# Order of VectorE's work between the expert chunks: the mixer's slices first, each routing step one chunk earlier

## The reference, cut to what matters

```python
def peer_ffn(xn, w_query, sub_keys, peer_u, peer_v):
    q = (xt @ w_query).reshape(t, PEER_HEADS, 2, PEER_HALF)
    sk = jnp.einsum('thcd,ckd->thck', q, sub_keys)
    top_s, top_i = lax.top_k(sk, PEER_TOPK)            # 16 of 128 keys, twice
    cand_s = top_s[:, :, 0, :, None] + top_s[:, :, 1, None, :]
    best_s, best_pos = lax.top_k(cand_s, PEER_TOPK)    # 16 of 256 pairs
    idx = jnp.take_along_axis(cand_i, best_pos, axis=-1)
    gate = jax.nn.softmax(best_s, axis=-1)
    h = einsum('thkd,td->thk', peer_u[idx], xt)
    return einsum('thk,thkd->td', gate * gelu(h), peer_v[idx])
x = x + y @ w_out                                      # end of the mixer
x = x + peer_ffn(rms_norm(x, norm2_g), w_query, sub_keys, peer_u, peer_v)
```

## Time and profile before

| what | value |
|---|---|
| median of 3 runs | 2962.0 us |
| profiled execution | 2951.57 us, span of its instructions 2949.8 us |
| busy: TensorE, VectorE, ScalarE, GpSimd | 2097.7, 2065.5, 1041.2, 1194.0 us |
| moved by DMA | 1173.26 MB, of which the gathers 1073.81 MB and the queue of weights 97.07 MB |
| first gather issued | at 160.3 us, the last at 2927.1 us |
| chain of work that ended last | gathers in flight 48%, TensorE 22%, VectorE 18% |

### The profile page before, as it was taken

The page is one execution under the profiler, slowest core; times in us unless marked ns, Lnnn a source line. Parts: engine busy times, 40 slices in busy tenths (PEclk is TensorE's granted clock), DMA queues, the critical chain, the costliest instruction groups (busy, mean ns, idle before and its releaser), DMA issues.

```text
span 2949.8 us, 37238 instructions
## 1 busy us (share of the span) xinstructions
PE 2097.7 (71%) x12696; PEld 1036.4 (35%) x12696; DVE 2065.5 (70%) x5215; ACT 1041.2 (35%) x3347; POOL 1194.0 (40%) x1028
## 2 busy tenths in 40 slices
PE   8888787777777876586775877667776665656565
PEld 7554454344443432243342533234343111111111
DVE  2466678977567687867567678976766766777665
ACT  2322345633233455423223345632223222222222
POOL 0034334443344334444343434543444444444443
PEclk9988999888888987888887988889898678677768
DMA  6189999999999999999999999999999999999998
GB/s 233 36 345 418 419 419 419 395 420 419 419 419 419 420 414 414 417 384 420 420 420 420 416 386 420 421 386 419 420 420 421 421 421 421 418 418 420 419 415 341
DMA packets 174350, 1173.26 MB, mean 398 GB/s; under 512 B 19280, under 2 KB 19408, under 8 KB 43088
## 3 DMA queue, kind: packets, MB, share of 16 engines
q0 software_dynamic: 147456, 1073.81, 87.8%
q1 hardware_dynamic: 26704, 97.07, 8.4%
HBM read 1168.71 MB, written 2.10 MB: 397 GB/s over the span
## 4 chain that ended last, share of the span: by engine, by line
DMA 48%; PE 22%; DVE 18%; ACT 5%; issue 5%; POOL 1%; SPq 0%; DVEq 0%; POOLq 0%; ACTq 0%
DMA gather<-experts,idx 48%; PE ysum L686 12%; DVE gather L1259 9%; PE bank L466 6%; ACT amp L915 2%; POOL gather L421 1%; ACT diag L923 1%; PE ysum L474 1%; PE bank L661 1%; ACT gel L908 1%; DVE x L1235 1%; PE bank L515 1%; DVE shared L1045 0%; DVE scratch L1206 0%; DVE scratch L1210 0%
## 5 line engine op out<-in xcount | busy, mean ns | idle before, releaser
L421 POOL DMA_INDIRECT gather<-experts,idx x1024 | 1193.8, 1166 | 1733.8 <-PE ysum L686 1411.5
L686 PE MATMUL ysum<-gather,diag 64*64 64x512 f32 x8192 | 1263.2, 769 | 728.3 <-ACT diag L923 696.7
L1259 DVE CUSTOM_DVE_ANT_0 gather<-gather,xc 128x1024 f32<-128x1024 f32 x1024 | 1229.8, 1224 | 682.8 <-DMA gather<-experts,idx 680.0
L686 PEld LDWEIGHTS ysum<-gather,diag 64*64 64x64 f32 x8192 | 365.7, 172 | 1526.9 <-ACT diag L923 906.8
L908 ACT ACTIVATE gel<-hdot 128x4 f32<-128x4 f32 x255 | 52.4, 205 | 1679.4 <-DVE hdot L1259 1679.4
L466 PE MATMUL bank<-xnT,w 128*128 128x256 f32 (+1 forms) x2048 | 467.1, 384 | 5.9 <-DVE xnT L975 5.9
L466 PEld LDWEIGHTS bank<-xnT,w 128*128 128x128 f32 x2048 | 380.0, 194 | 100.6 <-issue 42.8
L923 ACT ACTIVATE diag<-cc,amp 128x64 f32<-128x64 f32 x1020 | 267.9, 333 | 0.0
L915 ACT ACTIVATE amp<-gel,gate 128x1 f32<-128x1 f32 x1020 | 216.8, 283 | 8.3
L908 ACT ACT_TABLE_LOAD x105 | 134.7, 1283 | 1.8
L661 PEld LDWEIGHTS bank<-w,yT 128*128 128x128 f32 x768 | 87.3, 192 | 17.8 <-issue 17.8
(11 more groups left out here) (126 smaller groups left out, 1490.2 us busy)
## 6 DMA issues: line engine op xcount, KB each, us to landing
w<-weights SPq DMA_DIRECT2D x164, 512.0 KB, 7.9
gather<-experts,idx POOLq DMA_INDIRECT x1024, 15.1
gather<-weights SPq DMA_DIRECT2D x4, 1024.0 KB, 5.6
y_out<-x SPq DMA_DIRECT2D x4, 512.0 KB, 7.8
x<-x_in SPq DMA_DIRECT2D x2, 512.0 KB, 5.3
g2b<-g_rows SPq DMA_DIRECT2D x2, 512.0 KB, 11.7
x<-x_in SPq DMA_DIRECT2D x1, 1024.0 KB, 12.4
cc<-consts_in SPq DMA_DIRECT2D x1, 920.5 KB, 6.4
```

The source lines that it names most:

```text
L421: pool.indirect_dma_start(gather[:, n % SLOTS, :], None, uv_d[m // 2], bass.IndirectOffsetOnAxis(ap=idx[:, g % 2, k:k + 1], axis=0)).then_ ...
L686: mm = nc.tensor.matmul(ysum[outs, q * 512:(q + 1) * 512], diag[toks, n % NDIAG, :], gather[toks, n % SLOTS, DM + hf * 512:DM + (hf + 1) * ...
L1259: e = V.tensor_tensor_reduce(out=gather[:, n % SLOTS, 0:DM], in0=gather[:, n % SLOTS, 0:DM], in1=xc[:, :], scale=1.0, scalar=0.0, op0=ALU. ...
```

## The change

The routing step moves from ahead of the `yield` to behind it. On VectorE the order becomes: dot products of c, add_tile if due, slices of c, routing step, dot products of c + 1. And the steps of head g + 1 are assigned to other chunks: with g = cg // 4 + 1, `route_experts(g)` stands behind the slices of chunk 0 of head g - 1, `route_gate(g)` behind those of chunk 2, `route_keys(g + 1)` behind those of chunk 3. Only head 1, at the start, has its keys at chunk 0 and its experts at chunk 1 as before. The numbers and kinds of instructions do not change. The other engines' programs are as they were.

```diff
@@ peer_dve
-                head = c // 4
...
                     add_tile(cg // per_tile - 1)
-                nm, nh = divmod(m * TT * HEADS + head + 1, TT * HEADS)
-                if nm < NBLK:
-                    if c % 4 == 0:
-                        route_keys(dve, nm, nh)
-                    elif c % 4 == 1:
-                        route_experts(dve, nm, nh)
-                    elif c % 4 == 3:
-                        route_gate(dve, nm, nh)
-                yield
+                yield
+
+                g = cg // 4 + 1
+                route = lambda step, to: step(dve, *divmod(to, TT * HEADS)) if to < NBLK * TT * HEADS else None
+                if cg == 0:
+                    route(route_keys, g)
+                elif cg == 1 or c % 4 == 0:
+                    route(route_experts, g)
+                elif c % 4 == 2:
+                    route(route_gate, g)
+                elif c % 4 == 3:
+                    route(route_keys, g + 1)
             if m == NBLK - 1:
                 add_tile(m * TT + 1)
```

## The result

The changed kernel takes 2965.47 us (median of 7 runs, 2963.11 to 2970.89), the kernel before 2960.65 us in runs of the same session (7 runs, 2955.64 to 2963.01). The ratio is 1.002, with a 95% interval of 1.0011 to 1.0029. That is some 5 us: within the 0.3% that the forecast called no change and within its range, but the interval leaves one out, and the sign is not the one of the sum (-0.9 us). So there is a small loss to explain.

What follows compares the result with a forecast made beforehand. The DMA engines were taken to bound the kernel. The terms summed to -0.9 us, taking the runs' median of 2962.0 to 2961, and unplaced small waits to 2960.0 us; the range was 2944 to 2973.

Steps and rivals of the forecast that it cites:

- What bounds the kernel: Whole stream: the DMA engines bound it, so engine order can win only the time they lack work, 26.7 us.
- block 1's chunk 32: Slices ahead of the keys step let TensorE's spread start earlier: 2.5 us of gain, between 0 and 3.95.
- 1050 to 1240: Stretch of scattered dips losing 2.7 us, relieved ahead of chunk 2: taken as -1 us, between -2.7 and +3.
- the stretch 530 to 600: VectorE is the bound there, busy 68.10 of 70 us: taken as +1 us, between -2 and +4.
- the stretch with block 2's chunk 10: TensorE's wait for attention weights starts later, behind chunk 9: 0.4 us of cost, between -2.5 and +1.25.
- the one with chunk 33: Block 2: the chain behind chunk 33's dot products starts later, delayed by the experts step: cost 1.2 us, between 0 and 5.2.
- the six lossy stretches: Stretches below 420 GB/s between 530 and 2930 us, together losing 26.7 us, all the change can win in the stream.
- the shift by a chunk: Each head's steps a chunk earlier: zero in block 3; with slices, chunk 1's dot products 1.25 to 5.2 us later.
- rival B: Slower: keys and experts both ahead of chunk 1, some five places at 3 us, 2976 us; chance 0.10.
- The paragraph on waits: route_gate behind chunk 2 waits for gate_exp, which should be done in time; earlier indices are worth nothing in a full stream.
- The rule weighed: Gather issues beside dot products take up to 1 us more each: five starved places, at most +5 us, 2965 us.
- rival C: The port VectorE and GpSimd share slows gather issues beside dot products: 2965 us, not told from no change; chance 0.05.

Runs made afterwards that it cites:

- run 13: Kernel before, with only the head at chunk 32 of block 0 having its steps a chunk earlier, ahead of the slices: 2959.87 us, ratio 1.0011.
- Run 2: Changed kernel, with routing steps still a chunk earlier but put back ahead of the slices: 2962.15 us, ratio 1.002 to the kernel before.
- run 10: Kernel before, with only the first head of each tile (seven places) having its steps a chunk earlier: 2963.03 us, ratio 1.0021.
- run 6: Kernel before, steps at their old chunks, with slices first in every gap that does not hold the experts step: 2955.86 us, ratio 0.9998.
- run 3: Changed kernel, with routing ahead of the slices at chunk 12 of block 0 and chunk 0 of blocks 1 and 2: 2958.99 us, ratio 1.001.
- run 15: Changed kernel, with the first head of block 0's second tile at old places, its experts step ahead of the slices: 2964.09 us, ratio 1.0029.
- run 7: Kernel before, with only the keys step a chunk earlier and routing still ahead of the slices: 2955.06 us, ratio 1.0.
- run 9: Run 2 with the first head of each tile at its old places: 2958.16 us, ratio 1.0008 to the kernel before.
- run 11: Kernel before, with 3.84 us of dead VectorE work added ahead of chunk 0 of each tile, eight places: 2963.83 us, ratio 1.003.
- run 16: Kernel before, with the keys step alone a chunk earlier from block 1 on and block 0 left as before: 2951.57 us, ratio 0.9984.
- run 8: Run 2 with the experts step left behind chunk 1 at three heads (chunk 45 of block 0, 41 of blocks 1 and 2): 2961.45 us, ratio 1.0015.

## Why the prediction was right and wrong, point by point

*What bounds the kernel* was right. The DMA stream sets the time, and the change acted only through places where it ran dry.

*The terms with a size* came out near, in the changed kernel as a whole: block 1's chunk 32 -3.3 us (taken: -2.5), 1050 to 1240 -1.3 (-1), the stretch 530 to 600 +0.7 (+1), the stretch with block 2's chunk 10 +0.1 (+0.4), the one with chunk 33 +1.5 (+1.2), where TensorE's wait went from 9.02 to 10.49 us. Together -2.3 us, against a sum of -0.9. Some of that agreement is luck: the borders of the stretches decide tenths, and the dip of 530 to 600 runs on for another 1.2 us behind its border. The bounds of 530 to 600 went up to +4; run 13 shows 3.9 us there when the slices do not come first. The prediction's bounds, redone, add up to -11.2 and +13.5 us, not to -13 and +14; the range is hardly touched by it.

*The step that failed* is the one that gave the sum its sign. It had terms only for the six lossy stretches, "all that the change can win in the stream", and took the rest, at 419 and 420 GB/s, at nothing, for both parts of the change. For the order it gave a reason: "unplaced small waits ahead of TensorE's slices can only be relieved by the order". The full stretches could only lose, and did: 2.5, 4.3 and 3.9 us. Two causes meet there.

The first is *the shift by a chunk*. "Zero" was right for block 3 (still 420 GB/s), where nothing but routing fills the gaps. That the gaps ahead of chunk 1 would hold up to 5.2 us more with slices in them was seen; but outside the six stretches no term was made of it, and that it decides at the first heads of the tiles was left to rival B, with a chance of 0.10. Run 2 has the whole loss with the shift alone, and run 10 as much from seven heads. B's mechanism was right, and its places in part; its price, some 14 us, was two to three times too high, and it named none of the block starts.

The second is the order. The paragraph on waits asked only whether gate_exp would be done in time, which it was (GpSimd waited for indices 163.1 us in all, 162.7 of it ahead of the first gather). It never asked for whom VectorE's slices themselves wait. They wait for ScalarE's roots and TensorE's products, and the routing step ahead of them was the work that hid this: 2.89 us at each block start, 5.36 us behind chunk 12. Beside the old chunks this costs no time (run 6); in the changed kernel run 3 puts about half of the loss on it, with intervals that overlap.

*The rule weighed* (rival C) is not settled. The mean issue of a gather was 1167 ns against 1166, but a mean can't tell: five issues of 1 us more would raise it by 5 ns. At the new dips the rows are as C has them. In the changed kernel the first gather that GpSimd issues behind its long wait takes 1.79 us behind chunk 12 and 1.91 and 1.90 us at the two block starts, and the next one 1.99 each time; the same gathers took 1.37 us, and 0.93 or 0.94 the next one, in the kernel before. GpSimd at block 1's start, after:

```profile
927.03 1.91 POOL L421 DMA_INDIRECT gather<-experts,idx  x1 [10.93 <-PE ysum L686]
```

So a part of each new dip, some half a microsecond for the first gather and 1 us more for the second, can be C's, and no run separates it. Whether it is the sharing that the Trainium skill (SBUF — State Buffer, "SBUF: two separate sides") describes is not shown either.

*Not settled:* the shares within the changed kernel. Order and chunks interact (runs 13 and 15), the cases differ by 2 to 3 us, and that is the width of the intervals. Not settled either is block 0's second tile: up to its chunk 62 block 0 has lost 3.4 to 6 us in runs 2, 3, 7, 9, 10, 11 and 13, of which run 9 leaves the tile's first head as it was, and no run takes that apart.

## What to carry to other kernels

Before one step is put behind another, ask for both what they wait for: a step that looks like an obstacle ahead of the slice can be the filler of the slice's own wait. A stretch that already runs at the full rate is where a reordering can only lose, so list there how long the queue can be late and which engines fill it. If one part of a reordering has the gain and another the loss, test each by itself: here moving the keys step alone, and not in block 0, where it had cost 3.6 us, gave what the full change did not (0.9984 against 1.002).

## What the runs showed of the hardware that was not expected

The same program ahead of the stream does not take the same time: in the profiled runs the first gather was issued at 160.29, 163.13, 166.35 (run 13) and 167.43 us (run 16), with nothing changed before it. That is more than the effect of most of the experiments, so two single profiles compare only behind that point. And what an idle or busy VectorE costs in a stream bound by DMA is a matter of the place: at three places waits of over 6 us cost little that could be told (runs 2 and 8), 30.7 us of dead work cost 3 us in mid-tile, and 3.84 us of it at block 0's chunk 32 cost 3.9. Last, GpSimd's issue of a gather took 0.97 us in one row and 1.99 in another, the long one beside a dot product of VectorE.
